# A mixture-of-experts block on one core: moving the gather, the table load and the weight chunks

## The chip, the cores and the metric

The kernel runs on one core of a Trainium2 chip. The metric is the device time of one execution in microseconds (us), and the median over the runs counts.

## The reference

One layer for 256 tokens of width 1024, in float32. First come three gated branches (forgetting attention, a short convolution, cross-attention into a memory), then a mixture of 32 experts of which each token uses four:

```python
def moe(x2, w_router, b_router, w_up, b_up, w_down, b_down):
    logits = (x2 @ w_router + b_router).astype(jnp.float32)
    top_vals, top_idx = lax.top_k(logits, TOP_K)
    top_w = jax.nn.softmax(top_vals, axis=-1)
    combine = jnp.einsum('tk,tke->te', top_w,
                         jax.nn.one_hot(top_idx, N_EXPERTS, dtype=jnp.float32)).astype(x2.dtype)
    out = jnp.zeros_like(x2)
    for e in range(N_EXPERTS):
        a = clamped_swiglu(x2 @ w_up[e] + b_up[e])
        out = out + combine[:, e:e + 1] * (a @ w_down[e] + b_down[e])
    return out
```

`clamped_swiglu` splits its 2048 inputs into `glu` and `lin`, clamps both, and gives glu * sigmoid(1.702 glu) * (lin + 1). Each expert's w_up is 1024 x 2048 (8.4 MB) and w_down is 1024 x 1024 (4.2 MB), so the experts' weights are 403 MB.

## The kernel before

**Branches and router.** The first 270 us or so are the branches: weight pieces of 1 MB come through four `raw` buffers, are split into two parts and multiplied. Then x1 is transposed, the router's logits are computed, the top four experts chosen, and two tables built: for each token and expert its position in the expert's list (`pos_tab`) and its weight (`comb_tab`). Up to 64 tokens (SLOTS) are one *item*; an expert with more tokens gets further items behind the 32 of the regular loop (with the inputs at hand, no such item is seen in the trace).

**An item** is the function `item(n)`, once for each engine, and the five engines meet by semaphores only. The order of the work is written out by hand.

- TensorE (L1556 to 1644; the 32 items are unrolled): up products with k from 0 to 7, four matmuls for each k. `xgT[:, k]` is the stationary side; the 512-column pieces of the weight rows go in pairs into the two halves of the PSUM banks `bank_glu` and `bank_lin`. Each f32 matmul appears as two instructions in the trace. After k = 0 come the bias products (L1581). After k = 3 comes `gather(n + 1)` (L1494): the next expert's tokens are picked out of x1 with a 0/1 matrix `pick` scaled by the norm, into `bank_cy`. After k = 5 comes `turn_gathered(n + 1)` (L1506), four transposes of the gathered rows back into `bank_cy`. The last chunk (k = 6 and 7) is done for glu first and then for lin. Then come `scatter(n - 1)` (L1551), which adds the last item's result into four accumulator banks, the wait for the activation, four transposes into `bank_t` (L1613), the bias of the down products (L1619, behind a wait for `xg_ready` of n + 1), the down products m = 0 to 7 (L1631), and after m = 3 two transposes of `pick_w` into `bank_t` (L1642).
- VectorE (L1177 to 1205): clamp of glu (L1180), glu times sigmoid (L1183), clamp of lin (L1185), their product (L1189). Then `move_gathered(n + 1)` (L1125) makes `xgT` from `bank_cy`, `build_pick_w` and the next `build_pick` follow, then `pickT` and `slot_w` from the transposed pick_w (L1197, L1199), the next bias selection (L1122), and y_lo (L1204).
- ScalarE (L816 to 825): `copy_gathered(n + 1)` (L812) from `bank_cy` to `xg_tok`, sigmoid (L820), copy of aT (L822), y_hi (L825). In the loop an activation table is loaded before L812 and again before L820. `xg_tok` shares its memory with `sig`.
- SP issues the weight transfers (L437 to 448). The ring has 12 slots of 2 MB, 16 KB in each of 128 partitions. An expert has six chunks: four of w_up with two k each (UP_ROWS = 2), two of w_down with four m each. The ring holds two experts. Transfer g goes to slot g mod 12 when the chunk that was there has been used (`chunk_used`, L384 to 392). A chunk is read as `(p j) n -> p (j n)`, so each partition's part is one contiguous run.

**Before the loop** the ring's memory belongs to the branches. The first 12 transfers are therefore tied to the end of what lies there (L450 to 469): transfers 0 to 3 beside pieces 27, 29, 31 and 33, number 4 beside 35, number 5 behind the last proj block, 6 and 7 behind the splits of the last pieces (`lo_done`), 8 to 10 behind the last products (`half_used`), 11 behind the logits. `keep_up()` (L1471) puts four matmuls without use before the wait for the choice of experts, and again behind the first gather.

Of the kernel before, what the change touches and what calls it, by code (L numbers as in the profile page):

```python
# [5 lines left out]
F32 = mybir.dt.float32  # L6
F32R = mybir.dt.float32r
# [37 lines left out]
R_NEG, R_POS, R_END = 64, 96, 104  # L45

# [89 lines left out]
def hybrid_block(nc, x_d, mem_d, w_in, w_kv, w_branch, w_out, w_up, w_down,  # L136
                 cols_d, spread_d, wf_d, wr_d, b_gate, b_up, b_down, out):
    ctx = ExitStack()
    with ctx:
# [8 lines left out]
        slot_bytes = UP_ROWS * 2 * FF * 4  # L148
# [7 lines left out]
        ss = sb("ss", [P, 7, 16], F32)  # L156
        ms = sb("ms", [P, 16], F32)
        rstd = sb("rstd", [P, 7, 16], F32)
# [7 lines left out]
        iota_e = sb("iota_e", [32, 2], F32)  # L166
        meta = sb("meta", [1, EXTRA_COLS + 1], I32)
# [4 lines left out]
        start_m = start_ring + RING * slot_bytes  # L172
        ring = sb("ring", [P, RING, slot_bytes // 4], F32, Region(nc, start_ring, start_m))

        def in_slots(first, end):
            return Region(nc, start_ring + first * slot_bytes, start_ring + end * slot_bytes)

        u = in_slots(0, 4)
# [12 lines left out]
        v = in_slots(0, 1)  # L191
# [4 lines left out]
        r = in_slots(4, 5)  # L196
# [7 lines left out]
        r = in_slots(5, 6)  # L204
        yT_hi = [sb("y_fox_hi", [P, KB, SEQ], F32R, r), y_conv_hi, sb("y_mem_hi", [P, KB, SEQ], F32R, r)]
        yT_lo = [sb("y_fox_lo", [P, KB, SEQ], F32R, r), y_conv_lo, sb("y_mem_lo", [P, KB, SEQ], F32R, r)]
        raw = sb("raw", [P, 4, KB, W], F32, in_slots(6, 8))
        w_hi = sb("w_hi", [P, 4, 2, W], F32R, in_slots(8, 9))
        w_lo = sb("w_lo", [P, 4, 2, W], F32R, in_slots(9, 10))
        r = in_slots(10, 11)  # L210
# [3 lines left out]
        r = in_slots(11, 12)  # L214
# [7 lines left out]
        y = Region(nc, start_ring + 4 * slot_bytes, end_y)  # L222
# [48 lines left out]
        posT = sb("posT", [32, 2, NT, P], F32, t)  # L271
# [108 lines left out]
        def loads_of(slot, end):  # L380

            return sum(1 for g in range(end) if g % RING == slot)

# [39 lines left out]
        def _(sp):  # L423
# [26 lines left out]
            for p in range(1, NP):  # L450
# [4 lines left out]
                if p in (27, 29, 31, 33):  # L455
                    load_next((p - 27) // 2)
# [1235 lines left out]
```

## Time and profile before

| | us |
|---|---|
| median of 3 runs (1281.88 to 1283.11) | 1282.13 |
| the profiled execution | 1281.22 |
| its span, first to last instruction | 1279.4 |
| busy: TensorE matmuls | 1182.9 |
| busy: VectorE | 380.8 |
| busy: ScalarE | 313.6 |

The mean granted TensorE clock is 0.955 of 2.4 GHz. The core moves 450 MB, 352 GB/s over the span. Busy TensorE time is modelled from pipelined matmuls and says little about whether TensorE runs at its peak. What an item costs is read from the chain of waits, and how near the transfers are to their limit from stretches of GB/s.

### The profile page before, as it was taken

To read this page: it belongs to the slowest core of one execution; us is meant where nothing else is said; L and a number is where in the kernel's file an instruction comes from. 1 tells how busy PE (TensorE), PEld (TensorE's weight loads), DVE (VectorE), ACT (ScalarE), POOL (GpSimd) and SP (SyncE) were. 2 spreads that over 40 slices of the span, in tenths; PEclk is the share of its full clock that TensorE was granted. 3 is DMA by queue.
4 is the path that set the end of the run, shared out by engine and by line. 5 is a ranking of instruction groups with operands and counts; after the bars stand their busy time and mean duration, and the time that the engine had idled before them with its cause. 6 is when DMAs were issued, how large, how long until landed. Compare 5 with 4: busy or idle time off the path is not lost.

```text
span 1279.4 us, 13646 instructions
## 1 busy us (share of the span) xinstructions
PE 1182.9 (92%) x5596; PEld 549.9 (43%) x5596; DVE 380.8 (30%) x711; ACT 313.6 (25%) x432; POOL 80.2 (6%) x98
## 2 busy tenths in 40 slices
PE   8999999998999999999999998999999999999997
PEld 7789888863333333333333333333333333333332
DVE  5676855642211111111112122221111211211112
ACT  6655544431111111111111111111111111111111
POOL 6343320000000000000000000000000000000000
PEclk9999999999999999999999999999999999999998
DMA  8545489679999999999999999999999999999900
GB/s 298 166 139 178 145 302 381 226 309 376 411 411 410 411 410 413 410 411 411 410 410 407 416 408 407 411 417 401 411 413 412 405 404 407 410 412 409 412 37 33
DMA packets 51466, 449.99 MB, mean 352 GB/s; under 512 B 4610, under 2 KB 4738, under 8 KB 26836
## 3 DMA queue, kind: packets, MB, share of 16 engines
q1 hardware_dynamic: 49936, 447.76, 86.3%
q10 hardware_dynamic: 1476, 1.42, 0.4%
q8 instruction: 45, 0.74, 0.2%
q14 instruction: 9, 0.07, 0.0%
HBM read 448.12 MB, written 1.05 MB: 351 GB/s over the span
## 4 chain that ended last, share of the span: by engine, by line
PE 80%; DVE 10%; ACT 8%; issue 2%; POOL 1%; DMA 0%; DVEq 0%; ACTq 0%; SPq 0%; POOLq 0%
PE aux L1561 31%; PE aux L1631 22%; PE acc L1413 11%; PE aux L1494 5%; ACT L820 3%; PE acc L1406 3%; PE aux L1613 2%; DVE sig L1189 2%; DVE glu L1180 2%; DVE sig L1183 2%; PE aux L1506 2%; ACT sig L820 2%; DVE aux L1185 2%; ACT aT L822 2%; PE aux L1581 1%
## 5 line engine op out<-in xcount | busy, mean ns | idle before, releaser
L1561 PE MATMUL aux<-ring,xgT 128*64 128x512 f32 x2048 | 463.5, 594 | 0.8 <-DVE xgT L1129 0.8
L1631 PE MATMUL aux<-ring,aT 128*64 128x512 f32 x1024 | 288.0, 714 | 11.2 <-ACT aT L822 11.2
L1561 PEld LDWEIGHTS aux<-ring,xgT 128*64 128x64 f32 x2048 | 143.7, 137 | 264.3 <-issue 253.8
L1631 PEld LDWEIGHTS aux<-ring,aT 128*64 128x64 f32 x1024 | 80.0, 160 | 177.7 <-issue 157.0
L1180 DVE TENSOR_SCALAR glu<-aux 128x512 f32<-128x512 f32 x32 | 22.1, 691 | 418.9 <-PE aux L1561 418.9
L852 DVE TENSOR_TENSOR w_lo<-raw,w_hi 128x1024 fp32r<-128x1024 f32 x80 | 104.2, 1322 | 50.4 <-ACT w_hi L643 50.3
L643 ACT ACTIVATE w_hi<-raw 128x1024 fp32r<-128x1024 f32 x80 | 84.1, 1059 | 88.5 <-PE acc L1413 73.0
L825 ACT ACTIVATE y_hi<-aux,slot_w 128x512 fp32r<-128x512 f32 x32 | 22.0, 687 | 302.7 <-PE aux L1631 302.7
L820 ACT ACT_TABLE_LOAD x32 | 41.1, 1283 | 198.5 <-DVE glu L1180 198.5
L1613 PE MATMUL aux<-ident,sig 128*128 128x128 f32 x128 | 24.0, 310 | 70.0 <-DVE sig L1189 70.0
L1413 PE MATMUL acc<-w_hi,hT_hi 128*128 128x512 f32 x188 | 75.7, 403 | 1.4 <-DVE hT_lo L864 1.3
L812 ACT ACTIVATE sig<-aux 128x512 f32<-128x512 f32 x33 | 19.7, 597 | 231.5 <-PE aux L1494 231.5
L1413 PE MATMUL acc<-w_hi,hT_lo 128*128 128x512 f32 x188 | 73.3, 390 | 0.0
L1413 PE MATMUL acc<-w_lo,hT_hi 128*128 128x512 f32 x188 | 73.2, 390 | 0.0
L1197 DVE TENSOR_SCALAR pickT<-aux 128x256 fp32r<-128x256 f32 x32 | 13.6, 424 | 182.0 <-PE aux L1642 182.0
L1494 PE MATMUL aux<-x,pick 128*64 128x512 f32 x264 | 63.8, 605 | 0.7 <-DVE pick L1111 0.7
L1613 PEld LDWEIGHTS aux<-ident,sig 128*128 128x128 f32 x128 | 17.9, 209 | 84.4 <-DVE sig L1189 84.4
L822 ACT ACTIVATE aT<-aux 128x512 f32<-128x512 f32 x32 | 19.1, 597 | 97.4 <-PE aux L1613 97.4
L1183 DVE TENSOR_TENSOR sig<-glu,sig 128x512 f32<-128x512 f32 x32 | 22.2, 693 | 67.4 <-ACT sig L820 67.4
L812 ACT ACT_TABLE_LOAD x32 | 41.1, 1283 | 0.6
L1413 PEld LDWEIGHTS acc<-w_hi,hT_hi 128*128 128x128 f32 x188 | 35.3, 188 | 9.4 <-issue 1.6
L1413 PEld LDWEIGHTS acc<-w_hi,hT_lo 128*128 128x128 f32 x188 | 35.3, 188 | 7.6
(281 smaller groups left out, 1053.3 us busy)
## 6 DMA issues: line engine op xcount, KB each, us to landing
ring<-w_up_dram SPq DMA_DIRECT2D x128, 2048.0 KB, 12.3
ring<-w_down_dram SPq DMA_DIRECT2D x64, 2048.0 KB, 9.1
raw<-w_in_dram SPq DMA_DIRECT2D x25, 1024.0 KB, 5.2
raw<-w_branch_dram SPq DMA_DIRECT2D x6, 1024.0 KB, 5.2
raw<-w_kv_dram SPq DMA_DIRECT2D x4, 1024.0 KB, 5.2
raw<-w_out_dram SPq DMA_DIRECT2D x4, 1024.0 KB, 5.1
x<-x_dram SPq DMA_DIRECT2D x2, 512.0 KB, 4.1
raw<-w_in_dram SPq DMA_DIRECT2D x2, 512.0 KB, 5.9
```

The source lines that it names most:

```text
L643: nc.scalar.activation(w_hi[:, s % 4], raw[:, p % 4, 2 * h:2 * h + 2], ACT.Copy).then_inc(hi_done, 1)
L812: nc.scalar.activation(xg_tok[:], bank_cy[:], ACT.Copy).then_inc(xg_tok_ready, 1)
L820: nc.scalar.activation(sig[:], glu[:], ACT.Sigmoid, scale=ALPHA).then_inc(sig_ready, 1)
L822: nc.scalar.activation(aT[:].rearrange("p k s -> p (k s)"), bank_t[:], ACT.Copy).then_inc(aT_ready, 1)
L852: nc.vector.tensor_tensor(w_lo[:, s % 4], raw[:, p % 4, 2 * h:2 * h + 2], plain_f32(w_hi[:, s % 4]), ALU.subtract).then_inc(lo_done, 1)
L1180: nc.vector.tensor_scalar(glu[:], bank_glu[:], LIMIT, None, ALU.min).then_inc(glu_ready, 1)
L1183: nc.vector.tensor_tensor(sig[:], glu[:], sig[:], ALU.mult).then_inc(gated_ready, 1)
L1413: ins = nc.tensor.matmul(banks[t][:], a_[:, k, ts], w_, start=opening and m == 0 and kind != "gate", stop=closing and m == 2)
L1494: ins = nc.tensor.matmul(bank_cy[64 * half:64 * half + 64, :], pick[:, t], x1[:, t, half * W:(half + 1) * W], start=(t == 0), stop=(t == N ...
L1561: ins = nc.tensor.matmul(bank[64 * half:64 * half + 64, :], xgT[:, k], w_rows[:, c0 + half * W:c0 + (half + 1) * W], start=(k == 0), stop= ...
L1613: ins = nc.tensor.transpose(bank_t[:, j * P:(j + 1) * P], sig[:].rearrange("s (p j) -> s j p", j=DOWN_ROWS)[:, j], ident[:])
L1631: ins = nc.tensor.matmul(bank_cy[64 * half:64 * half + 64, :], aT[:, j, 64 * ff_half:64 * ff_half + 64], w_rows[:, half * W:(half + 1) * W ...
```

## The change

- TensorE: `gather(n + 1)` moves from behind k = 3 to behind the scatter, so that it runs before the wait for the activation. The pick_w transposes move from between the down products to directly behind the four aT transposes, and go to `bank_lin`. `turn_gathered` moves from behind k = 5 to behind down product m = 1, and goes to `bank_glu`. The bias of the down products waits for `xg_tok_ready` (the copy of the gathered rows) in place of `xg_ready`. The next item's up products wait for `pickT_ready`. The last two k go glu first as before, now inside a chunk.
- ScalarE: a sigmoid of one column opens each item; `copy_gathered` moves behind the real sigmoid.
- VectorE: `build_pick_w` waits for `gathered`; `move_gathered` moves behind the two readings of the transposed pick_w.
- Transfers: w_up comes in two chunks of 4 MB, 32 KB per partition, in place of four of 2 MB; w_down stays. The ring still has 12 units of 2 MB, now as eight chunks in the pattern 2, 2, 1, 1. The first two w_up chunks are loaded in halves, beside pieces 27 to 33 as before. One 4 MB transfer on the condition of the last piece takes the place of numbers 6 and 7.
- `keep_up` has 8 matmuls before the choice, 4 new ones before the first gather and 3 behind it (before: 4, none and 4). The wait for `extra_ready` moves ahead of the first turn.
- Memory: `xg_tok`, `pick`, `pick_w`, `ones_f` and `posT` get places of their own, apart from `sig`; `ss` and `rstd` are packed (an offset `STAT[n]` in place of a row of 16).

The diff without the renaming of slots to units and without the packing of `ss` and `rstd`:

```diff
...
@@ -28,11 +28,14 @@
 TABLE = NEXP + EXTRA_COLS + 4
-UP_ROWS, DOWN_ROWS = 2, 4
+UP_ROWS, DOWN_ROWS = 4, 4
 UP_CHUNKS, DOWN_CHUNKS = KD // UP_ROWS, KD // DOWN_ROWS
 CHUNKS = UP_CHUNKS + DOWN_CHUNKS
-RING = 12
-WARM_UP, KEEP_UP = 14, 4
+UNITS, CHUNK_UNITS = 12, (2, 2, 1, 1)
+RING = 2 * CHUNKS
+FIRST_UNIT = [UNITS // 2 * (s // CHUNKS) + sum(CHUNK_UNITS[:s % CHUNKS]) for s in range(RING)]
+HALVED = 2
+WARM_UP, KEEP_UP = 14, (8, 4, 3)
 NEG, HUGE = -1.0e30, 3.0e38
...
@@ -241,21 +248,23 @@
         xgT = sb("xgT", [P, KD, SLOTS], F32, m)
+        start_aT = m.at
         aT = sb("aT", [P, KB, P], F32, m)
-        start_t = m.at
+        start_y_hi = m.at
         y_hi = sb("y_hi", [P, W], F32R, m)
+        start_y_lo = m.at
         y_lo = sb("y_lo", [P, W], F32R, m)
+        end_y_lo = m.at
         m = Region(nc, start_gate, end_gate)
         sig = sb("sig", [P, W], F32, m)
-        xg_tok = sig
-
-        m = Region(nc, start_gate, end_gate - 4 * W)
-        pick_w = sb("pick_w", [P, NT, 2, SLOTS], F32, m)
-        pick = sb("pick", [P, NT, SLOTS], F32, m)
-        ones_f = sb("ones_f", [32, P], F32, m)
-
-        t = Region(nc, start_t, start_gate)
+
+        xg_tok = sb("xg_tok", [P, W], F32, Region(nc, start_y_hi, start_y_lo))
+        pick_w = sb("pick_w", [P, NT, 2, SLOTS], F32, Region(nc, start_y_lo, end_y_lo))
+        ones_f = sb("ones_f", [32, P], F32, Region(nc, start_gate, end_gate))
+
+        posT = sb("posT", [32, 2, NT, P], F32, Region(nc, start_aT, start_y_hi))
+        t = Region(nc, start_y_lo, end_y_lo)
         logits = sb("logits", [P, NT, NEXP], F32, t)
...
@@ -379,7 +387,12 @@
-            return sum(1 for g in range(end) if g % RING == slot)
+            return sum(1 for g in range(end) if g % RING == slot) + (1 if slot < HALVED else 0)
+
+        def chunk_tile(slot):
+
+            units = slice(FIRST_UNIT[slot], FIRST_UNIT[slot] + CHUNK_UNITS[slot % CHUNKS])
+            return ring[:, units].rearrange("p u n -> p (u n)")
@@ -434,6 +447,13 @@
+            def load_half_chunk(g, half):
+                rows = UP_ROWS // 2
+                n = rows * 2 * FF
+                src = w_up[0, g * UP_ROWS * P:(g + 1) * UP_ROWS * P, :].rearrange("(p j) n -> p j n", p=P)
+                sp.dma_start(chunk_tile(g)[:, half * n:(half + 1) * n],
+                             src[:, half * rows:(half + 1) * rows]).then_inc(slot_loaded[g], 16)
+
@@ -442,7 +462,7 @@
                     src = w_down[bass.ds(expert, 1), c * n:(c + 1) * n, :].rearrange("o (p j) n -> p (o j n)", p=P)
-                sp.dma_start(ring[:, slot], src).then_inc(slot_loaded[slot], 16)
+                sp.dma_start(chunk_tile(slot), src).then_inc(slot_loaded[slot], 16)
@@ -453,20 +473,20 @@
                 if p in (27, 29, 31, 33):
-                    load_next((p - 27) // 2)
+                    n = (p - 27) // 2
+                    load_half_chunk(n // 2, n % 2)
                 if p == 35:
                     sp.wait_ge(half_used, 2 * LAST_PIECE[("proj", 1, 1)] + 2)
-                    load_next(4)
+                    load_next(2)
             sp.wait_ge(half_used, 2 * LAST_PIECE[("proj", 0, 1)] + 2)
+            load_next(3)
+            sp.wait_ge(lo_done, 2 * NP)
+            load_next(4)
+            sp.wait_ge(half_used, 2 * NP)
             load_next(5)
-            for g, last in ((6, NP - 3), (7, NP - 1)):
-                sp.wait_ge(lo_done, 2 * last + 2)
-                load_next(g)
-            sp.wait_ge(half_used, 2 * NP)
-            for g in (8, 9, 10):
-                load_next(g)
+            load_next(6)
             sp.wait_ge(logits_ready, 1)
-            load_next(11)
+            load_next(7)
             for g in range(RING, NEXP * CHUNKS):
...
@@ -814,10 +834,10 @@
             def item(n):
-                copy_gathered(n + 1)
-                act.wait_ge(xg_turned, n + 1)
+                nc.scalar.activation(ms[:, 0:1], minus_half[:, 0:1], ACT.Sigmoid)
                 act.wait_ge(glu_ready, n)
                 nc.scalar.activation(sig[:], glu[:], ACT.Sigmoid, scale=ALPHA).then_inc(sig_ready, 1)
+                copy_gathered(n + 1)
                 act.wait_ge(aT_done, n)
...
@@ -1127,7 +1147,7 @@
                 nc.vector.tensor_tensor(xgT[:].rearrange("p (h q) s -> p q h s", h=2),
-                                        bank_cy[:].rearrange("p (q h s) -> p q h s", q=KD // 2, h=2),
+                                        bank_glu[:].rearrange("p (q h s) -> p q h s", q=KD // 2, h=2),
                                         gain.to_broadcast([P, KD // 2, 2, SLOTS]), ALU.mult).then_inc(xg_ready, 1)
@@ -1189,14 +1209,15 @@
-                move_gathered(n + 1)
+                dve.wait_ge(gathered, n + 1)
                 build_pick_w(bass.ds(n - 1, 1))
...
                 dve.wait_ge(pick_wT_done, n)
-                nc.vector.tensor_scalar(pickT[:].rearrange("p t s -> p (t s)"), bank_t[:, 0:NT * P], 0.0, None,
+                nc.vector.tensor_scalar(pickT[:].rearrange("p t s -> p (t s)"), bank_lin[:, 0:NT * P], 0.0, None,
                                         ALU.is_gt)
-                nc.vector.tensor_reduce(slot_w[:], bank_t[:, 0:NT * P], AX, ALU.add).then_inc(pickT_ready, 1)
+                nc.vector.tensor_reduce(slot_w[:], bank_lin[:, 0:NT * P], AX, ALU.add).then_inc(pickT_ready, 1)
+                move_gathered(n + 1)
                 dve.wait_ge(y_done, n)
@@ -1468,11 +1489,11 @@
-            def keep_up():
-                for _ in range(KEEP_UP):
+            def keep_up(stretch):
+                for _ in range(KEEP_UP[stretch]):
                     nc.tensor.matmul(acc[0][:], ones_bf[0:96], bias_up[:, 0:W], start=True, stop=True)
-            keep_up()
+            keep_up(0)
             pe.wait_ge(chosen_ready, 1)
@@ -1503,11 +1524,13 @@
                     rows = xg_tok[:, c * n:(c + 1) * n].rearrange("s (p j) -> s j p", j=UP_ROWS)[:, j]
-                    ins = nc.tensor.transpose(bank_cy[:, q * P:(q + 1) * P], rows, ident[:])
+                    ins = nc.tensor.transpose(bank_glu[:, q * P:(q + 1) * P], rows, ident[:])
                 ins.then_inc(xg_turned, 1)
+            keep_up(1)
             gather(1)
-            keep_up()
+            keep_up(2)
+            pe.wait_ge(extra_ready, 1)
             turn_gathered(1)
...
@@ -1564,9 +1587,9 @@
                 pe.wait_ge(xg_ready, n)
-                if first_item:
-                    pe.wait_ge(extra_ready, 1)
-                for k in range(KD - UP_ROWS):
+                if not first_item:
+                    pe.wait_ge(pickT_ready, n - 1)
+                for k in range(KD - 2):
                     c, j = k // UP_ROWS, k % UP_ROWS
@@ -1588,24 +1611,14 @@
-
-                    if k == 3:
-                        if not first_item:
-                            pe.wait_ge(y_hi_ready, n - 1)
-                            pe.wait_ge(y_lo_ready, n - 1)
-                        gather(n + 1)
-                    if k == 5:
-                        turn_gathered(n + 1)
-
-                c = UP_CHUNKS - 1
-                pe.wait_ge(slot_loaded[slot_of[c]], loads[c])
                 for bank, c0, done in ((bank_glu, 0, glu_done), (bank_lin, FF, up_done)):
-                    for k in range(KD - UP_ROWS, KD):
+                    for k in range(KD - 2, KD):
                         ins = up_product(k, bank, c0)
...
                     scatter(n - 1, second_item)
+                gather(n + 1)
                 pe.wait_ge(a_ready, n)
@@ -1614,7 +1627,13 @@
-                pe.wait_ge(xg_ready, n + 1)
+                pe.wait_ge(pick_w_ready, n)
+                for t in range(NT):
+                    ins = nc.tensor.transpose(bank_lin[:, t * P:(t + 1) * P],
+                                              pick_w[:, t].rearrange("p a s -> p (a s)"), ident[:])
+                ins.then_inc(pick_wT_done, 1)
+
+                pe.wait_ge(xg_tok_ready, n + 1)
                 for half in range(2):
...
@@ -1636,16 +1655,12 @@
                         ins.then_inc(slot_used[slot], 1)
-                    if m == 3:
-                        pe.wait_ge(pick_w_ready, n)
-                        for t in range(NT):
-                            ins = nc.tensor.transpose(bank_t[:, t * P:(t + 1) * P],
-                                                      pick_w[:, t].rearrange("p a s -> p (a s)"), ident[:])
-                        ins.then_inc(pick_wT_done, 1)
+                    if m == 1:
+                        turn_gathered(n + 1)
...
                 chunks = range(CHUNKS * (n - 1), CHUNKS * n)
-                item(n, [g % RING for g in chunks], [16 * (g // RING + 1) for g in chunks], n == 1, n == 2)
+                item(n, [g % RING for g in chunks], [16 * loads_of(g % RING, g + 1) for g in chunks], n == 1, n == 2)
             more = pe.value_load(meta[0:1, EXTRA_COLS:EXTRA_COLS + 1], min_val=0, max_val=EXTRA)
...
```

## Rows read from the trace of the kernel before

**Rows 1.** Page: GB/s read and written in 40 equal slices of the span

```profile
GB/s 298 166 139 178 145 302 381 226 309 376 411 411 410 411 410 413 410 411 411 410 410 407 416 408 407 411 417 401 411 413 412 405 404 407 410 412 409 412 37 33
```

**Rows 2.** Chain of waits over one item: start us, us, engine, tile, line, instructions

```profile
702.89 0.70 DVE glu L1180
...
703.66 1.28 ACT L820
...
707.84 0.76 PE aux L1613 x4
...
708.62 0.61 ACT aT L822
...
709.28 5.35 PE aux L1631 x16
714.63 0.37 PE aux L1642 x2
715.00 3.58 PE aux L1631 x16
718.58 1.72 PE aux L1561 x8
...
725.88 1.72 PE aux L1494 x8
...
731.03 0.67 PE aux L1506 x4
...
733.62 0.70 DVE glu L1180
```

**Rows 3.** Timeline of the same item: last scatter products, bias products

```profile
705.29 0.40 PE L1551 MATMUL acc<-y_lo,pickT 64*128 64x512 f32 x2
...
708.52 0.41 PE L1619 MATMUL aux<-bias_down,bias_sel 96*64 96x512 bf16 x2
```

**Rows 4.** Stretches: busy us of the engines, granted clock, DMA share, GB/s

```profile
710.00:710.50 0.50, 0.50 (x4) 0.24 (x2) 0.00 (x0) 0.00 (x0) 0.00 (x0) 0.50 1.08 459
277.00:304.00 27.00, 24.55 (x122) 9.34 (x122) 7.86 (x39) 3.01 (x5) 0.00 (x0) 0.94 1.01 429
718.00:745.00 27.00, 24.50 (x114) 8.67 (x110) 5.23 (x11) 5.08 (x6) 0.00 (x0) 0.94 1.01 428
779.50:806.50 27.00, 24.50 (x114) 8.63 (x110) 5.23 (x11) 5.08 (x6) 0.00 (x0) 0.94 1.01 423
340.00:1215.00 875.00, 804.55 (x3646) 282.25 (x3646) 169.88 (x371) 144.61 (x171) 0.00 (x0) 0.94 0.99 410
530.00:540.00 10.00, 10.00 (x50) 3.52 (x50) 1.74 (x4) 1.97 (x2) 0.00 (x0) 1.00 0.93 365
```

**Rows 5.** Waits of the DMA-issuing queue, 500 to 1250 us: total, times, longest us

```profile
SPq L445 <- PE aux L1561: 352.7, 92, 4.8
SPq L445 <- PE aux L1631: 310.2, 47, 9.7
```

**Rows 6.** Chain of waits in item 1, and the last down products of item 32

```profile
292.00 1.87 PE aux L1561 x8
...
303.36 0.70 DVE glu L1180
...
1268.05 3.61 PE aux L1631 x16
```

**Rows 7.** Ring transfers issued near 262 and 272 to 277 us, and time to landing

```profile
L445 SPq DMA_DIRECT2D ring<-w_up_dram x1: 328/328/328, 262.4 to 262.4; - x1
DMA to landing us min/median/max: 7.7/7.7/7.7
...
L445 SPq DMA_DIRECT2D ring<-w_down_dram x2: 328/380/432, 272.7 to 276.7; - x2
L445 SPq DMA_DIRECT2D ring<-w_up_dram x1: 432/432/432, 272.2 to 272.2; - x1
DMA to landing us min/median/max: 13.5/18.0/18.8
```

More of the change, by code:

```diff
@@ L45 @@
 R_NEG, R_POS, R_END = 64, 96, 104
+STAT = [0, 2, 4, 20, 36, 44, 52, 56]
 def blocks_and_pieces():
@@ L166, in hybrid_block @@
         iota_e = sb("iota_e", [32, 2], F32)
+        pick = sb("pick", [P, NT, SLOTS], F32)
         meta = sb("meta", [1, EXTRA_COLS + 1], I32)
@@ L171, in hybrid_block, with in_units @@
         start_ring = always.at
[L172 to L178, printed above, removed]
+        start_m = start_ring + UNITS * unit_bytes
+        ring = sb("ring", [P, UNITS, unit_bytes // 4], F32, Region(nc, start_ring, start_m))
+        def in_units(first, end):
+            return Region(nc, start_ring + first * unit_bytes, start_ring + end * unit_bytes)
+        u = in_units(0, 4)
         mT_hi = sb("mT_hi", [P, KD, SEQ], F32R, u)
@@ L203, in hybrid_block @@
         rden = sb("rden", [P, 2, 2], F32, r)
[L204 removed]
+        r = in_units(5, 6)
         yT_hi = [sb("y_fox_hi", [P, KB, SEQ], F32R, r), y_conv_hi, sb("y_mem_hi", [P, KB, SEQ], F32R, r)]
         yT_lo = [sb("y_fox_lo", [P, KB, SEQ], F32R, r), y_conv_lo, sb("y_mem_lo", [P, KB, SEQ], F32R, r)]
[L207 to L210, printed above, removed]
+        raw = sb("raw", [P, 4, KB, W], F32, in_units(6, 8))
+        w_hi = sb("w_hi", [P, 4, 2, W], F32R, in_units(8, 9))
+        w_lo = sb("w_lo", [P, 4, 2, W], F32R, in_units(9, 10))
+        r = in_units(10, 11)
         hT_lo = sb("hT_lo", [P, KD, SEQ], F32R, r)
@@ L610, in _ @@
             pool.wait_ge(x1_squared, 4)
-            halves = ss[:, 6, 0:2 * NT].rearrange("p (t h) -> p t h", h=2)
+            halves = ss[:, STAT[6]:STAT[6] + 2 * NT].rearrange("p (t h) -> p t h", h=2)
             chained(nc.gpsimd.tensor_tensor(ms[:, 0:NT], halves[:, :, 0], halves[:, :, 1], ALU.add))
             chained(nc.gpsimd.tensor_scalar(ms[:, 0:NT], ms[:, 0:NT], 1.0 / D, NORM_EPS, ALU.mult, ALU.add))
-            nc.gpsimd.tensor_tensor(rstd[:, 6, 0:NT], ms[:, 0:NT], minus_half[:, 0:NT], ALU.pow
+            nc.gpsimd.tensor_tensor(rstd[:, STAT[6]:STAT[6] + NT], ms[:, 0:NT], minus_half[:, 0:NT], ALU.pow
                                     ).then_inc(rstd_ready, 1)
@@ L647, in _ @@
                 act.wait_ge(x_loaded[t], 16)
-                nc.scalar.activation(xs[:, t], x1[:, t], ACT.Square, accum_out=ss[:, 0, t:t + 1]
+                nc.scalar.activation(xs[:, t], x1[:, t], ACT.Square, accum_out=ss[:, STAT[0] + t:STAT[0] + t + 1]
                                      ).then_inc(ss_ready[0], 1)
@@ L774, in _ @@
                         act.wait_ge(mem_loaded[t], 16)
-                        ins = nc.scalar.activation(scratch[t], mem_sb[:, t], ACT.Square, accum_out=ss[:, 1, t:t + 1])
+                        ins = nc.scalar.activation(scratch[t], mem_sb[:, t], ACT.Square, accum_out=ss[:, STAT[1] + t:STAT[1] + t + 1])
                     ins.then_inc(ss_ready[1], 1)
@@ L1110, in build_pick @@
                 for t in range(NT):
-                    ins = nc.vector.tensor_scalar(pick[:, t], iota[:], pos_tab[:, t, col], rstd[:, 6, t:t + 1],
+                    ins = nc.vector.tensor_scalar(pick[:, t], iota[:], pos_tab[:, t, col], rstd[:, STAT[6] + t:STAT[6] + t + 1],
                                                   ALU.is_equal, ALU.mult)
@@ L1558, in up_product @@
                 def up_product(k, bank, c0):
-                    w_rows = ring[:, slot_of[k // UP_ROWS]].rearrange("p (j n) -> p j n", j=UP_ROWS)[:, k % UP_ROWS]
+                    w_rows = chunk_tile(slot_of[k // UP_ROWS]).rearrange("p (j n) -> p j n", j=UP_ROWS)[:, k % UP_ROWS]
                     for half in range(2):
@@ L1626, in item @@
                     slot = slot_of[c]
-                    w_rows = ring[:, slot].rearrange("p (j n) -> p j n", j=DOWN_ROWS)[:, j]
+                    w_rows = chunk_tile(slot).rearrange("p (j n) -> p j n", j=DOWN_ROWS)[:, j]
                     if j == 0:
```

35 lines of the change are left out of this document (17 added, 18 removed).

## The prediction

> **What bounds the kernel now.** I read the page first [rows 1]. The span is 1279.4 us, and the slices of 32 us show a plateau near 410 GB/s that breaks off two slices before the end. For the last 64 us or so nothing is loaded while the experts still run. The expert part is 32 items, each reading 12.6 MB of weights, and the loads are finished about two items before the arithmetic. Two items are exactly what the ring holds. So the ring is full in the steady state and TensorE sets the pace, although the transfers are close behind it.
>
> Then I read the chain of waits over one item [rows 2]. It comes back to the same point (the clamp of the glu half, L1180) after 733.62 - 702.89 = 30.73 us. Two stretches of it are not matmuls. The first runs from 702.89 to 707.84, 4.95 us: clamp on VectorE, 1.28 us for an activation table, sigmoid, three VectorE steps. The second is the copy of aT on ScalarE, 0.61 us. Everything else is TensorE in a row: up products, with the gather (1.72) and the turning of the gathered rows (0.67) laid between them, and down products with the pick_w transposes (0.37) between their halves.
>
> The timeline shows what TensorE does in the first stretch [rows 3]. The lin half of the last up products runs on for 1.72 us (eight instructions, as at 718.58 in [rows 2]), to 704.58, and the scatter ends at 705.69, so the scatter is 1.11 us. Then TensorE is idle until 707.84, 2.15 us. At 710 its granted clock is at 0.50, which is 1.2 GHz [rows 4], and the first 16 down instructions take 5.35 us against 3.58 us for the second 16 [rows 2]: 1.77 us per item lost to the clock.
>
> The queue's own waits say the same from the other side [rows 5]: SP spends 663 us of a 750 us stretch waiting until TensorE frees a slot. But look at what is in flight. While transfers are queued the core reads 429, 428 and 423 GB/s, and its mean over 875 us is 410 [rows 4]. TensorE is first by only some 4%. That second bound decides this change.
>
> **The change, part by part.** TensorE first, per item.
> - Gather (1.72) goes out of the up stream into the gap behind the scatter. The up stream up to the glu half is then 733.62 - 718.58 - 1.72 - 0.67 = 12.65 us, the turn having moved as well.
> - The table load (1.28) moves to the head of the item, on ScalarE beside up products that last 12.65 us. The chain of the activation becomes 4.95 - 1.28 = 3.67 us. If the load stayed where it is, the chain would be 4.95 again.
> - TensorE's own work in the gap is now 1.72 (lin) + 1.11 (scatter) + 1.72 (gather) = 4.55 us, longer than 3.67. So the stall is covered. What is late next is TensorE itself. If the load came back, the wait would be 0.4 us.
> - VectorE now waits for the gather before pick_w and the next pick. Behind it stand pickT and move_gathered, wanted only at the next item: nothing is charged. ScalarE copies the gathered rows (0.6) behind the sigmoid, before aT. They are ready at 4.55, the copy ends at 5.2, and the aT transposes end at 4.55 + 0.76 = 5.3, so it fits.
> - Behind the aT transposes come pick_w's transposes (0.37) and the bias product (0.41): 0.78 us of work over the 0.61 us aT copy, so that wait vanishes too.
> - The turn (0.67) now sits behind the second down product, visible as before. Down is 2 x 3.58 + 0.67 = 7.83 us if the clock stays up, which I assume because no idle time precedes it.
>
> Sum for TensorE: 12.65 + 4.55 + 0.76 + 0.37 + 0.41 + 7.83 = 26.6 us against 30.73, a gain of 4.2 us per item. If TensorE set the pace this would be 130 us.
>
> Transfers. They cannot follow. The bytes are the same, in 192 units of 2 MB (2,097,152 bytes). The mean of the three stretches with a full queue is 426.7 GB/s, or 4.915 us a unit and 29.5 us an item. 26.6 is below that, so the ring drains and from some item on TensorE waits for weights. It starts with a lead. Item 1 reaches its glu clamp at 303.36 [rows 6], 2.39 us earlier without gather and turn, and ends 4.55 + 0.76 + 0.78 + 7.83 us later, at 314.9. Item 2 wants its second up chunk at 322, and that is in at 286, since all of expert 2 is in at 276.7 + 18.8 = 295.5 [rows 7]. The lead of 35 us melts by 2.9 us an item, so the waits begin at about item 14. From there the end is set by the transfers alone.
>
> Early loads. The first four ring transfers become halves of two chunks, in the same places, bytes and queue positions. Two 2 MB transfers, the second of them issued at 262.4, become one of 4 MB on that later condition. The old one landed 7.7 us after issue [rows 7]; 4.9 more gives 275.0. The next ones are released by 272.7, so the queue stays filled and catches up. Cost nothing. If that cover failed, it would be one unit, 4.9 us.
>
> Coarser frees. The first slot of item 1 comes free after four k instead of two, at 292.00 + 1.87 = 293.9 [rows 6]. A transfer of 4 MB issued then lands at 293.9 + 7.7 + 4.9 = 306.5. A queue that never ran short would give 295.5 + 9.8 = 305.3, so I charge 1.2 us. The second slot comes at 302.7 and could land from 315.3, before its turn at 316.3: nothing. Later TensorE is faster than the transfers and slots are free in time. The other keep-up products before and behind the first gather shift item 1 by under 2 us either way, so the charge lies between 0 and 3 us.
>
> 32 KB per partition in place of 16 KB. No row shows it. Taken from both sides, the rate lies between the lowest 10 us of the steady state, 365 GB/s, and one unit per 4.8 us, the closest two landings (290.7 and 295.5) [rows 7], which is 437. I take 426.7, since the same queue at 16 KB is nearest.
>
> **The sum.** Transfers end at 295.5 + 1.2 + 180 x 4.915 = 1181.4. The second up chunk of expert 32 is in two units earlier, at 1171.6. Behind it TensorE needs 3.44 (k 4 and 5) + 1.72 (glu) + 4.55 + 0.76 + 0.37 + 0.41 + 7.83 = 19.1 us, so the last product ends at 1190.7. From there to the end was 1279.4 - 1271.66 = 7.7 us [rows 6] and nothing in it changes: span 1198.4. The profiled execution took 1281.22, which is 1.8 over its span, and the median of the runs is 0.9 above that: **1201 us**.
>
> **Rivals.**
> A. *410 GB/s is the ceiling, not TensorE's pace.* The plateau is flat at 410 and the DMA share there is 0.99. Against it: within an item the rate exceeds it for 27 us on end. A unit then takes 5.115 us, transfers end at 1217, the total is 1237. Even so the kernel gains, because the two items of lead are eaten up.
> B. *Longer runs, or a queue that never empties, lift the rate to the best landing distance*, 4.8 us a unit: transfers end at 1160.7, total 1181. For it: landings of 4.8 exist. Against: others of 5 us and more lie between them even with the queue full, since the long stretches average 426.7. The Trainium skill (DMA: Bandwidth & Descriptors, Where 436 GB/s comes from) puts a ceiling of 435 GB/s on the 16 ports, and measures 425 for one large transfer; at 435 the total would be about 1184 by that page, and the trace's long stretches agree with its 425 instead.
> C. *TensorE stays the bound.* Waits for weights take the place of the old idle time, and the clock drops twice per item: 26.6 + 2 x 1.77 = 30.1 us. With item 1 ending at 314.9 that makes 314.9 + 31 x 30.1 + 7.7 + 2.7 = 1258. Against it: a TensorE that slow isn't made to wait, so the drops would stop.
> D. *The other side: the w_up transfers run slower at 32 KB per partition.* Sixteen engines then read addresses twice as far apart. This decides from 5.59 us a unit for w_up, 375 GB/s: (1262.4 - 296.7 - 60 x 4.915) / 120, where 1262.4 is the end of the transfers that gives 1282. At 365 GB/s [rows 4] it is 5.75 us, transfers end at 1281 and the total is 1301, slower than before. For it only that the rate does sink to 365 in single windows; but those are at the point where the queue has run short once per item, with a DMA share of 0.93. The Trainium skill (DMA: Bandwidth & Descriptors, Latency and other measured facts) reports losses for row pitches of large powers of two, but from 2 MB up, and almost none at 512 KB; by it a pitch of 32 KB costs nothing. No row here shows it.
>
> **Chances.** Forecast 0.70 (own range 1192 to 1212: 423 to 429 GB/s, one clock drop in the last item, up to 5 us of early gaps), A 0.10, B 0.10, C 0.05, D 0.05. The range 1182 to 1226 leaves out C, D, the outer part of A and the edge of B, about 0.2. Less than 0.2% (2.6 us) can't be told from no change. Faster 0.95; slower 0.04; same 0.01, the piece of D near its point of decision.
>
> **What would show it.** Right: SP no longer waits for TensorE in the second half; TensorE or its weight loads wait for w_up transfers after about item 14, once or twice an item, some 2.9 us in all; GB/s near 426 in every slice until about 17 us before the end; items 2 to 12 spaced 26.6 us, later ones 29.5; one table load per item, none in the chain; gather inside the gap. A clock below full before item 14 would make the TensorE sum wrong without moving the time. Wrong: a plateau at 410 (A) or 435 (B); SP still waiting at the end and the loads done two items early (C); w_up transfers alone landing over 5.6 us apart per 2 MB (D).

## The result and the profile after

The changed kernel takes 1201.47 us (median of 4 runs, 1200.95 to 1202.44) against 1282.21 us (four runs, one more than in the table before): ratio 0.937, interval 0.9354 to 0.9386, a gain of 80.7 us. Forecast were 1201 us and a range of 1182 to 1226. The profiled execution took 1201.8 us with a span of 1200.0. All figures below are of fast executions; one slow one of late_table, at 1924 us, is left out.

From the page of the changed kernel: GB/s in 40 slices, three costly groups and the w_up transfers.

```profile
GB/s 318 146 176 145 159 223 359 312 193 407 434 428 428 431 427 433 427 430 431 424 435 425 430 430 428 434 422 433 429 427 430 429 430 425 432 427 430 428 430 115
...
L1584 PE MATMUL aux<-ring,xgT 128*64 128x512 f32 x2048 | 469.7, 608 | 39.2 <-DMA ring<-w_up_dram 38.4
...
L1650 PE MATMUL aux<-ring,aT 128*64 128x512 f32 x1024 | 232.2, 595 | 0.0
...
L837 ACT ACT_TABLE_LOAD x32 | 41.1, 1283 | 0.6
...
ring<-w_up_dram SPq DMA_DIRECT2D x62, 4096.0 KB, 49.7
```

Beside [rows 1], the plateau is at 422 to 435 GB/s instead of 410 and reaches into the last slice but one. The lead of two items is gone. TensorE, which before waited for no weights, stood idle 38.4 us for w_up transfers. The group of the down products (L1650, before L1631) has fallen from 288.0 us of busy time on the page before to 232.2 at the same count: that is the 1.77 us of slow clock per item. A w_up transfer now lands 49.7 us after its issue, for 4 MB; on the page before it was 12.3 us for 2 MB.

The chain of waits over one item, early in the loop (start, us, engine, tile, line, instructions), to set beside [rows 2]:

```profile
339.01 1.72 PE aux L1584 x8
...
341.16 12.02 PE aux L1584 x56
353.18 1.12 PE acc L1574 x8
354.30 1.89 PE aux L1515 x8
...
357.01 0.44 PE aux L1632 x2
...
357.78 1.72 PE aux L1650 x8
...
365.48 0.85 PE aux L1584 x3
```

The item is 365.48 - 339.01 = 26.47 us long and TensorE has work in nearly all of it. The clamp, the sigmoid and the table are no longer in the chain. One small wait stands in it: between the end of the gather (356.19) and the pick_w transposes (357.01) VectorE makes pick_w. The four aT transposes run beside it, and 0.17 us of idle time is left in each item, 5.2 us in all (total, times, longest us):

```profile
PE aux L1632 <- DVE pick_w L1137: 5.2, 31, 0.2
```

Later the waits come. TensorE's timeline around the first of them, and the stretch that answers to the 410 GB/s of [rows 4]:

```profile
630.50 1.94 PE L1584 MATMUL aux<-ring,xgT 128*64 128x512 f32 x8 [0.18 <-DMA ring<-w_up_dram]
...
640.12 7.09 PE L1584 MATMUL aux<-ring,xgT 128*64 128x512 f32 x32 [2.10 <-DMA ring<-w_up_dram]
...
669.38 8.79 PE L1584 MATMUL aux<-ring,xgT 128*64 128x512 f32 x32 [2.12 <-DMA ring<-w_up_dram]
```

```profile
340.00:1150.00 810.00, 769.14 (x3654) 278.30 (x3652) 175.02 (x368) 113.89 (x171) 0.00 (x0) 0.99 1.00 429
```

The first of the three is at the start of item 14 (630.50 us). After a wait of 2.1 us the clock drops in some items and not in others: the same 32 instructions take 7.09 us at 640 and 8.79 us at 669. What decides it no run shows.

The end of the chain, to set beside [rows 6]:

```profile
1163.74 5.15 PE aux L1584 x24
1168.89 2.17 another core or an unknown queue
...
1171.10 8.78 PE aux L1584 x32
...
1186.91 5.33 PE aux L1650 x24
```

```profile
1171.10:1172.10 1.00, 1.00 (x6) 0.43 (x8) 0.00 (x0) 0.00 (x0) 0.00 (x0) 1.00 0.81 344
1172.20:1175.20 3.00, 3.00 (x8) 0.73 (x6) 0.00 (x0) 0.00 (x0) 0.00 (x0) 0.50 0.60 257
```

The row of 2.17 us without a name is the wait for the last 4 MB of w_up, in at 1171.06. The two stretches under the chain (last three columns: granted clock, DMA share, GB/s) show the clock: still full in the first microsecond after the wait, then at half (1.2 GHz) for about three. TensorE ends 21.2 us after the landing, at 1192.24, and the span 7.8 us after that.

### The profile page after: what moved, and what is told of

It is laid out like the page before. It is cut to its first block, busy times and chain, and to the rows that moved or that the text cites. A ratio compares the mean times of both kernels' runs of the same rounds, so it can differ in the third digit from the quotient of the medians.

```text
span 1200.0 us, 13568 instructions
## 1 busy us (share of the span) xinstructions
PE 1142.9 (95%) x5603; PEld 545.4 (45%) x5603; DVE 386.8 (32%) x711; ACT 279.0 (23%) x432; POOL 81.1 (7%) x98
## 4 chain that ended last, share of the span: by engine, by line
PE 72%; DMA 21%; DVE 3%; another core or an unknown queue 2%; issue 1%; ACT 1%; POOL 0%; DVEq 0%; SPq 0%; POOLq 0%; ACTq 0%
PE aux L1584 29%; DMA ring<-w_up_dram 21%; PE acc L1434 14%; PE aux L1650 13%; PE aux L1515 3%; PE acc L1427 3%; PE acc L1574 2%; PE aux L1527 1%; PE aux L1604 1%; PE aux L1632 1%; DVE pick_w L1137 1%; DVE w_lo L872 1%; PE aux L1638 1%; DMA x<-x_dram 0%
## 5 line engine op out<-in xcount | busy, mean ns | idle before, releaser
L1584 PE MATMUL aux<-ring,xgT 128*64 128x512 f32 x2048 | 469.7, 608 | 39.2 <-DMA ring<-w_up_dram 38.4
L1584 PEld LDWEIGHTS aux<-ring,xgT 128*64 128x64 f32 x2048 | 152.1, 140 | 332.0 <-issue 276.0
L1650 PE MATMUL aux<-ring,aT 128*64 128x512 f32 x1024 | 232.2, 595 | 0.0
L1650 PEld LDWEIGHTS aux<-ring,aT 128*64 128x64 f32 x1024 | 68.6, 136 | 115.5 <-issue 110.0
L839 ACT ACTIVATE sig<-glu 128x512 f32<-128x512 f32 x32 | 20.2, 630 | 413.4 <-DVE glu L1200 413.4
L1142 DVE TENSOR_SCALAR bias_sel<-ones_bf,exp_sel 96x64 bf16<-96x64 bf16 x33 | 7.8, 236 | 151.3 <-PE aux L1650 151.3
L832 ACT ACTIVATE xg_tok<-aux 128x512 f32<-128x512 f32 x33 | 19.7, 598 | 109.6 <-PE aux L1515 109.6
L1149 DVE TENSOR_TENSOR xgT<-aux,cols 128x512 f32<-128x512 f32 x33 | 22.8, 692 | 64.5 <-PE aux L1527 64.5
L837 ACT ACT_TABLE_LOAD x32 | 41.1, 1283 | 0.6
L1434 PEld LDWEIGHTS acc<-w_lo,hT_hi 128*128 128x128 f32 x188 | 35.6, 189 | 7.1
L1137 DVE TENSOR_SCALAR pick_w<-iota,pos_tab,comb_tab 128x128 f32<-128x128 f32 x64 | 19.3, 344 | 40.3 <-PE aux L1515 40.3
L1574 PE MATMUL acc<-y_hi,pickT 64*128 64x512 f32 x128 | 28.7, 444 | 1.8 <-DVE y_lo L1225 1.8
## 6 DMA issues: line engine op xcount, KB each, us to landing
ring<-w_up_dram SPq DMA_DIRECT2D x62, 4096.0 KB, 49.7
```

The costliest lines, as they stand in the source:

```text
L837: nc.scalar.activation(ms[:, 0:1], minus_half[:, 0:1], ACT.Sigmoid)
L1137: ins = nc.vector.tensor_scalar(pick_w[:, t], iota[:].unsqueeze(1).to_broadcast([P, 2, SLOTS]), pos_tab[:, t, col], comb_tab[:, t, col], A ...
L1149: nc.vector.tensor_tensor(xgT[:].rearrange("p (h q) s -> p q h s", h=2), bank_glu[:].rearrange("p (q h s) -> p q h s", q=KD // 2, h=2), ga ...
L1434: ins = nc.tensor.matmul(banks[t][:], a_[:, k, ts], w_, start=opening and m == 0 and kind != "gate", stop=closing and m == 2)
L1574: ins = nc.tensor.matmul(acc[2 * t + half][:], pickT[s, t], part[s, :], start=opening and part is y_hi, stop=True, skip_group_check=True)
L1584: ins = nc.tensor.matmul(bank[64 * half:64 * half + 64, :], xgT[:, k], w_rows[:, c0 + half * W:c0 + (half + 1) * W], start=(k == 0), stop= ...
```

## The experiments

All ratios are to the kernel before, in runs on the same chip in turn.

### The bound of the kernel before

*before_32k*, the transfer half of the change, in the old order:

```diff
-UP_ROWS, DOWN_ROWS = 2, 4
+UP_ROWS, DOWN_ROWS = 4, 4
...
-RING = 12
+UNITS, CHUNK_UNITS = 12, (2, 2, 1, 1)
+RING = 2 * CHUNKS
...
```

> The order of work before, with w_up in 4 MB chunks of 32 KB per partition: the transfer half of the change alone. If TensorE sets the pace of the kernel before (my theory), the item stays at 30.73 us and the time at 1282 within 2 us, with the loads again done two items before the end. If the 410 GB/s seen before was what the transfers could do with 16 KB, the longer runs would show as a shorter time: at 429 GB/s an item would take 29.3 us and the total would be some 1235.

*half_before* loads only half of the bytes of experts 3 to 32 and multiplies old weights for the rest:

```diff
...
+                if isinstance(expert, int) and expert >= 2:
+                    half = dst.shape[1] // 2
+                    dst, src = dst[:, 0:half], src[:, 0:half]
...
```

> The kernel before with the same halved transfers (experts 3 to 32 bring the first half of each partition's run; the rest of the weights used is old). If TensorE set its pace, nothing changes: 1282 within 1 us, items of 30.7 us. If the transfers held it up in any way, by their rate or by crowding the memory ports, it is faster; at the rival's worst, 410 GB/s as a ceiling, it would fall to whatever TensorE can do alone.

Measured: before_32k 1282.75 us, ratio 0.9999 (0.9989 to 1.0008); half_before 1283.22 us, ratio 1.0001 (0.9992 to 1.0010). The stretch from 340 to 1150 us of half_before (busy us of the engines, granted clock, DMA share, GB/s):

```profile
340.00:1150.00 810.00, 743.59 (x3366) 261.77 (x3368) 158.79 (x347) 132.65 (x157) 0.00 (x0) 0.94 0.61 204
```

Half the bytes, 204 GB/s, and no less time. The transfers did not set the pace of the kernel before. The chain of an item did: TensorE's work and the activation that it waits for. The transfer half of the change alone is worth nothing. Rival A is out: 410 GB/s was TensorE's pace.

### The bound of the kernel after

*half_after* is the changed kernel with the same three lines.

> The changed kernel, in which the transfers of experts 3 to 32 bring only the first half of each partition's run, so that half of the weights used there are old ones in the ring. This takes the bound of the transfers away. TensorE alone then sets the pace: item 1 ends at 312.5, 31 more of 26.5 us, 7.8 behind them and 1.8 around the span: 1143, with no wait for a transfer and a granted clock near 1.0. If what is left after the change is not the transfers' doing but TensorE's (clock drops, own work), it stays at 1201.

Measured: 1143.15 us, ratio 0.891 (0.8896 to 0.8924), with no wait for a transfer in the trace:

```profile
340.00:1100.00 760.00, 755.28 (x3676) 273.95 (x3672) 175.65 (x369) 114.82 (x172) 0.00 (x0) 1.00 0.65 235
```

This is the forecast 1143 to a fraction of a microsecond. The change would be worth 140 us if weights came at will. The transfers keep 58 us of it.

The other side, matmuls without use in *work8* and *work18* (`range(8)` and `range(18)`):

```diff
                     pe.wait_ge(meta_ready, 1)
+                for _ in range(8):
+                    nc.tensor.matmul(bank_t[:], ones_bf[0:96], bias_up[:, 0:W], start=True, stop=True)
                 for j in range(DOWN_ROWS):
```

> The changed kernel with eight matmuls without use (0.215 us each) ahead of the aT transposes of each item: 1.7 us more TensorE work, 28.2 us an item. That is below the transfers' 29.3 us, so only the last item's share shows at the end: 1203. If TensorE's time still counted in each item, it would be 1201 + 32 x 1.7 = 1256.

> The same with 18 such matmuls, 3.9 us more, 30.4 us an item. Now TensorE is the slower one again: item 1 ends at 316, 31 more of 30.4 and 9.6 us around them give 1268, with no waits for weights. If the transfers had more slack or less than 29.3 us an item, the two kernels with added work would not bracket it in this way.

Measured: work8 1201.93 us, ratio 0.9375 (0.9359 to 0.9391); work18 1262.94 us, ratio 0.9851 (0.9834 to 0.9867). The chain of work8, then that of work18:

```profile
342.35 1.72 PE aux L1584 x8
...
370.41 1.72 PE aux L1584 x8
```

```profile
333.63 3.99 PE aux L1626 x18
...
346.69 1.72 PE aux L1584 x8
...
376.93 1.72 PE aux L1584 x8
```

Items of 370.41 - 342.35 = 28.06 us cost next to nothing in total. Items of 376.93 - 346.69 = 30.24 us set the time again. The turning point is not at the 29.5 us that the transfers need for an item (6 units of 4.912 us, see below) but under it, since TensorE starts behind a full ring. In the changed kernel item 1 ends at 312.5 and item 32 at 1192.2, so 31 items have 28.4 us each. Items of 28.06 us are just below that: work8 waits for weights in its last six items only, 6.7 us in all.

I had expected 1268 for work18 by adding 3.9 us to each item. It has no wait for pick_w any more, and an item grew by 3.77 us, to 30.24 in place of 30.4: 31 times 0.16 us are the 5 us.

### Which part of the change did it

*before_table* adds one instruction to the kernel before:

```diff
                 copy_gathered(n + 1)
+                nc.scalar.activation(ms[:, 0:1], minus_half[:, 0:1], ACT.Sigmoid)
                 act.wait_ge(xg_turned, n + 1)
```

> The kernel before with only a one-column sigmoid behind its copy of the gathered rows, so that the table is loaded ahead of the clamp of glu. The idle time of TensorE in each item falls from 2.15 to 0.87 us. If the clock still drops behind it, an item takes 30.73 - 1.28 = 29.45 us and the total is 1241. If the shorter pause keeps the clock at 2.4 GHz, the item's own work is 27.7 us, the transfers take over as the bound, and the total is 1200 to 1206, nearly all of the change's gain from one line.

Measured: 1200.03 us, ratio 0.9355 (0.9339 to 0.9370). That is the whole gain of the change; the two intervals overlap (0.9354 to 0.9386 for the change). ScalarE's timeline in one item, TensorE's first aT transposes of that item, and the chain:

```profile
356.38 1.28 ACT L818 ACT_TABLE_LOAD   x1
357.68 0.20 ACT L818 ACTIVATE ms<-minus_half 128x1 f32<-128x1 f32 x1
```

```profile
365.41 0.75 PE L1614 MATMUL aux<-ident,sig 128*128 128x128 f32 x4 [0.87 <-DVE sig L1190]
```

```profile
361.74 0.70 DVE glu L1181
...
362.53 0.64 ACT sig L821
...
365.41 0.77 PE aux L1614 x4
...
366.85 3.65 PE aux L1632 x16
...
389.50 0.70 DVE glu L1181
...
1126.80 48.90 DMA ring<-w_up_dram
...
1175.74 1.96 PE aux L1562 x8
```

The table is loaded at 356.38, 6 us before the sigmoid at 362.53. TensorE's pause before the transposes is 0.87 us instead of 2.15 [rows 2, 3]. The first 16 down instructions take 3.65 us instead of 5.35. The item is 389.50 - 361.74 = 27.76 us: 1.28 us for the load and 1.70 us for a clock that stays at 2.4 GHz. That is already below the turning point (28.4 us above; 28.1 here, from the end of item 1 at 318.9 to that of item 32 at 1190.4). The queue stays full at 428 GB/s, from item 26 on the items are 28.8 to 29.4 us apart, and the end hangs on the last w_up transfer, in at 1126.80 + 48.90 = 1175.70:

```profile
340.00:1150.00 810.00, 769.90 (x3702) 275.49 (x3700) 170.76 (x371) 152.50 (x202) 0.00 (x0) 1.00 1.01 428
```

Gather, pick_w transposes and turning, the larger part of the diff, bring an item from 27.76 to 26.47 us, where some 28.1 to 28.4 are enough. On top of the table load they shorten nothing that counts here. Whether they would have been enough without it is not shown: that takes a changed kernel with the load in the chain, and the next two runs did not give one.

*late_table* was meant to put the load back into the chain:

```diff
             def item(n):
-                nc.scalar.activation(ms[:, 0:1], minus_half[:, 0:1], ACT.Sigmoid)
                 act.wait_ge(glu_ready, n)
```

> The changed kernel without the one-column sigmoid, so that the table is loaded again behind the clamp of glu. In the items before TensorE waits for weights, the chain of the activation is 4.95 us against 4.55 us of TensorE work in the gap: items of 27.0 to 27.3 us instead of 26.5. The transfers need 29.3 us an item, so the total stays at 1201.5 plus at most 1 us for the last item. The rival, that this load is worth its full 1.28 us in each item, gives 1201.5 + 41 = 1242.

*exp_head* was the second attempt, with `ACT.Exp` in the place of `ACT.Sigmoid` on the line removed above:

> The changed kernel with an exponential of one column at the head of each item where it has a sigmoid. The table at the head is then the wrong one, and a second load must come behind the clamp of glu, as in the kernel before (late_table did not bring it back: its single load stayed at the head). The chain of the activation becomes 4.95 us against 4.55 us of TensorE work, so items before the waits for weights take 26.9 to 27.3 us. The transfers need 29.3 us: total 1201 plus at most 1 us. The rival, the load's full price in every item, gives 1242.

Measured: late_table 1199.27 us (three runs), ratio 0.9356 (0.9338 to 0.9374); exp_head 1200.91 us, ratio 0.9357 (0.9341 to 0.9373). The totals are as expected, but neither kernel tests what it was made for. ScalarE's timeline of exp_head:

```profile
369.27 1.28 ACT L837 ACT_TABLE_LOAD   x1
370.56 0.20 ACT L837 ACTIVATE ms<-minus_half 128x1 f32<-128x1 f32 x1
370.77 1.28 ACT L839 ACT_TABLE_LOAD   x1
381.68 0.63 ACT L839 ACTIVATE sig<-glu 128x512 f32<-128x512 f32 x1 [9.63 <-DVE glu L1200]
```

and of late_table:

```profile
366.38 1.28 ACT L838 ACT_TABLE_LOAD   x1
378.79 0.63 ACT L838 ACTIVATE sig<-glu 128x512 f32<-128x512 f32 x1 [11.13 <-DVE glu L1199]
```

The second load does come, but at 370.77, directly behind the one-column exponential, and waits there for no one. The sigmoid comes after the clamp some 11 us later. In late_table the single load stayed at the head of the item as well. So in the changed order the load is out of the chain with or without the one-column instruction. In the kernel before, two waits (`xg_turned`, `glu_ready`) stood ahead of the sigmoid and the load came behind them; here there is one. That this is the reason was not tried.

### The length of the runs, and the end

*w16* and *w16_again*: the changed kernel with 2 MB chunks of w_up.

```diff
-UP_ROWS, DOWN_ROWS = 4, 4
+UP_ROWS, DOWN_ROWS = 2, 4
...
-UNITS, CHUNK_UNITS = 12, (2, 2, 1, 1)
+UNITS, CHUNK_UNITS = 12, (1, 1, 1, 1, 1, 1)
...
```

The early loads are those of the kernel before again.

> The changed kernel with w_up again in 2 MB chunks of 16 KB per partition and twelve slots: the order half of the change alone. If the length of the runs does nothing for the rate (429 GB/s with a full queue), it is not slower, and gains where chunks are finer: 3.4 us at the end, where TensorE can start on k 4 and 5 of the last expert before k 6 and 7 are in, and 1.2 us at the first free slot: 1197. If the 0.6% by which the measured rate lies over the one read before (429.3 against 426.7 GB/s) comes from the 32 KB runs, 180 transfers take 5 us more and that gain is lost again: 1202.

> The same kernel as w16 (16 KB runs). If the run length is worth 0.5% of the rate, it shows 427 GB/s again where the changed kernel shows 429 and lands its last w_up chunk some 4 us later, and its total is 1200.5, since the finer last chunk gives 3 to 4 us back. If the two rates are alike here, its total is 1197.

*after_again*, without an edit:

> The changed kernel once more, beside the three below on the same chip: 1201.5 within 1 us, 429 GB/s with a full queue and a granted clock of 0.98 to 0.99. It gives the yardstick for w16: if w16's 427 GB/s was the chip's and not the 16 KB runs', this one shows 427 as well.

Measured: w16 1200.46 us, ratio 0.9356 (0.9344 to 0.9369); w16_again 1200.38, ratio 0.9358 (0.9345 to 0.9371); after_again 1201.06, ratio 0.9366 (0.9352 to 0.9379). The stretches from 340 to 1150 us show 427 GB/s for w16_again and 429 for after_again and for the changed kernel. Landings say it more exactly. For w16_again, then for the changed kernel, the issue of unit 24 and of the last one, each with its time to landing:

```profile
L465 SPq DMA_DIRECT2D ring<-w_down_dram x1: 328/328/328, 339.2 to 339.2; - x1
...
DMA to landing us min/median/max: 15.4/15.4/15.4
...
L465 SPq DMA_DIRECT2D ring<-w_down_dram x2: 4246/4248/4249, 1129.2 to 1133.5; - x2
...
DMA to landing us min/median/max: 50.2/50.5/50.8
```

```profile
L465 SPq DMA_DIRECT2D ring<-w_down_dram x1: 328/328/328, 339.0 to 339.0; - x1
...
DMA to landing us min/median/max: 16.7/16.7/16.7
...
L465 SPq DMA_DIRECT2D ring<-w_down_dram x1: 327/327/327, 1130.7 to 1130.7; - x1
...
DMA to landing us min/median/max: 50.2/50.2/50.2
```

With 16 KB runs unit 24 is in at 339.2 + 15.4 = 354.6 and unit 192 at 1184.3: 4.939 us a unit. With 32 KB runs it is 355.7 and 1180.9: 4.912 us. The other traces in which the transfers set the pace agree: 4.939 (w16) and 4.925 (before_table) with 16 KB, 4.903 to 4.912 in the five others with 32 KB. So the coarser transfers are 0.3 to 0.7% faster, and the last one is in 3.4 us earlier here. Run length, size and number of the transfers change together, and no run tells which of them counts. At unit 24 the changed kernel is 1.1 us behind. Not the later free slot does that, but the early loads: its first twelve units are in at 276.8 + 20.4 = 297.2, those of w16_again at 277.0 + 18.6 = 295.6, before a slot is used again. The finer chunks give the rest back at the end, where TensorE can start on k 4 and 5 earlier. The totals are equal within what can be told. My either-or of w16 was wrong in that both halves hold.

*split_end*: only the last w_up chunk of expert 32 in two halves.

```diff
...
+                for half, done in ((0, slot_loaded[g % RING]), (1, tail_loaded)):
+                    sp.dma_start(chunk_tile(g % RING)[:, half * n:(half + 1) * n],
+                                 src[:, half * (UP_ROWS // 2):(half + 1) * (UP_ROWS // 2)]).then_inc(done, 16)
...
+                if last_item:
+                    pe.wait_ge(tail_loaded, 16)
...
```

> The changed kernel, in which only the last w_up chunk of expert 32 comes in two halves with a semaphore each. TensorE, which stood still from 1168.9 to 1171.1 for the whole chunk, can go on with k 4 and 5 at once. By the theory that the end is the last transfer plus TensorE's work behind it, the last product ends 2.2 us of waiting and some 1.9 us of slow clock earlier: 1197.4. If something else than this chunk sets the end (the w_down chunks, or the scatter), nothing changes: 1201.5.

Measured: 1198.64 us (1197.98 to 1199.20), ratio 0.9345 (0.9331 to 0.9358), the fastest kernel of the study, 2.4 us below after_again in the same runs. Its chain in item 32, then that of after_again:

```profile
1164.13 12.02 PE aux L1596 x56
```

```profile
1172.05 7.09 PE aux L1584 x32
```

All 56 instructions run through in 12.02 us, where the changed kernel has 5.15 + 2.17 + 8.78. I had expected a gain of 4.1 us. The waiting of 2.2 us is gone; the 1.9 us of slow clock are not there to be gained in each execution, for after_again ran its last 32 up instructions in 7.09 us with no drop.

## Why the prediction was right

- *TensorE sets the pace before, the transfers are 4% behind.* Right, and shown by half_before and before_32k, if TensorE's pace means the item's chain with the activation in it.
- *26.6 us of TensorE work an item.* 26.47 measured. The gap was 4.73 us (1.72, 1.12, 1.89) against 4.55, the up stream 12.45 against 12.65, the down part 7.70 against 7.83. I charged nothing for VectorE's wait for the gather; it leaves TensorE idle for 0.17 us, 0.06 of them beyond the sum (0.82 us from the gather to the pick_w transposes in place of 0.76).
- *The transfers take over at about item 14 and set the end.* The first wait stands at the start of item 14, and the last w_up chunk was in at 1171.06 against 1171.6 in the sum. The first slot's 4 MB landed at 292.6 + 14.3 = 306.9 (forecast 306.5), but that agreement is luck. The early loads, charged at nothing, brought the first twelve units in at 297.2 in place of 295.5. The later free slot, charged at 1.2 us, cost nothing: its transfer was issued at 292.6, before those were in, and landed 9.7 us after them, two units at the full rate. The last transfer landed at 1180.9 (1181.4), a unit took 4.912 us (4.915). The last agreement hides two small errors: the stretches of GB/s that I read the rate from stand 0.5% above what the landings give (4.939 us with 16 KB, so 424.6 GB/s), and the coarser transfers, charged at nothing, are 0.3 to 0.7% faster. Item 1 ended at 312.5 in place of 314.9, which with the transfers as the bound changes nothing. The Trainium skill (DMA: Bandwidth & Descriptors, Where 436 GB/s comes from) has a ceiling of 435 GB/s and 425 for one large transfer; the trace agrees with the second, 427 by the landings.
- *TensorE needs 19.1 us behind the last w_up chunk.* 21.2 measured, the term that was most off. In the item's last up products the clock dropped 1 us after the wait, and 32 instructions took 8.78 instead of 6.88 us. That drop stood in the forecast's own range, not in its sum, and it is the difference between 1198.4 and 1200.0 us of span. In after_again it did not come: from the last chunk (1172.0) to TensorE's end (1191.5) are 19.5 us.
- *What would show it: SP no longer waits for TensorE.* Wrong. The queue's waits in the same stretch as [rows 5]:

```profile
SPq L465 <- PE aux L1584: 346.7, 44, 10.6
SPq L465 <- PE aux L1650: 255.7, 44, 8.6
```

602 us of the 631 to its last issue at 1130.7 are waiting, against 663 of 710 before. SP issues far ahead and always waits for the next slot, whoever is the slower one. The sign that tells the two states apart is the time from issue to landing, 49.7 against 12.3 us, and who waits for the data.
- *The table load is 1.28 us, and the stall is covered by the gather behind it.* The sizes were right, the weight was not. The forecast summed all parts and so never asked which of them is enough. The load alone, with the clock that it had been costing, is enough to leave the end to the transfers. Of the load's price, the Trainium skill (ScalarE: Activation LUTs, What ACT_TABLE_LOAD costs) gives 1283 ns and a drain of some 1380 ns besides. The trace agrees with the first. Of the second nothing shows here: from the clamp's end at 703.59 to the sigmoid at 704.95 [rows 2] it is the load and 0.08 us.
- Rivals: A (410 a ceiling) is refuted by half_before and by 429 GB/s in the stretch above; B (437 GB/s, 4.8 us a unit) by the landings (its 4.8 came of rows rounded to 0.1 us: the two landings are 4.89 us apart in the trace); C (TensorE stays the bound) by half_after and work8; D (w_up slower at 32 KB) by 4.912 against 4.939 us a unit.

## What to carry to other kernels

Where two bounds lie 4% apart, work out both for every part of a change: here one instruction took the kernel to the second bound, and everything beyond it was work at a place that no longer counts. Count the lead in: with two items in a full ring TensorE must be down to 28.4 us an item, not 29.5, before the transfers alone set the end. Halving the bytes and adding work without use are two cheap runs that say which bound holds and how much room there is. A pause of TensorE costs more than its length if the clock drops behind it, so the first microsecond to remove is the one that ends the drop.

## What the runs showed of the hardware beyond that

- **A pause of 0.87 us left the clock alone, one of 2.15 us did not.** Each stands before the same four transposes and a 0.35 us wait (before_table, with a granted clock of 1.00 from 340 to 1150 us, and the kernel before, with 0.50 at 710). Waits of 2.1 us for weights had both outcomes, 7.09 and 8.79 us for the same 32 instructions.
- **The profiled execution of w16 ran at a granted clock of 0.95 throughout**, with no drops in the loop, and its items took 27.5 us instead of 26.5 (chain of waits, gather to gather, 523.52 to 551.05). The stretch from 340 to 1150 us:

```profile
340.00:1150.00 810.00, 789.23 (x3674) 276.36 (x3672) 175.88 (x370) 114.82 (x172) 0.00 (x0) 0.95 1.01 427
```

Its total was 1201.8 us against 1200.1 to 1200.6 for the kernel's other four executions: 4% more TensorE time per item for 0.1% of the total. It says once more that TensorE is not the bound there. What set this clock no run shows.
- **An activation table can be loaded long before the instruction that needs it**, 11 us ahead in exp_head and 12 in late_table, before the wait (`glu_ready`) that the program places ahead of that instruction is over.
- **With 9 to 11 ring transfers issued and not yet landed, a single issue on SP can take 1.2 to 11.8 us** in place of 0.33: 98 of them in w16_again (4.2 us in the lines above), 69 in w16, 47 in before_table. The changed kernel never has more than 7 on the way, and none of its issues is long. The landings of w16_again are on average 4.94 us a unit before the first such issue (588 us) and 4.93 behind it, so it cost no time here.
